# Heads of an RWKV-7 trunk: three waits placed anew (a maximum, a wait for a Newton step, a one-column sigmoid)

## The chip, the core and the metric
One core of one Trainium2 chip runs the whole program. The metric is the device time of one execution in microseconds (us); of several runs the median is taken. PE is the matrix engine (TensorE), DVE is VectorE, ACT is ScalarE, POOL is GpSimd, SP only issues DMAs.

## What is computed
Two layers (DEPTH = 2) of a trunk run over 544 tokens, 512 of a prompt and 32 of a second request. Of each layer this matters here:

```python
x = LN1(ALPHA*x + 0.5*swiglu_1(x))
u, z = split(x @ w_in)                    # z: r, k, v of 12 heads x 64, and low-rank inputs
w = -softplus(-(w0 + tanh(lw) @ w2)) - 0.5; decay = exp(-exp(w)); a = sigmoid(a0 + la @ a2)
kk = k*k_k; kk = kk / max(sqrt(sum(kk*kk)), 1e-12)      # key norm, per head
for t: S = S*w_t + (S a_t) b_t + v_t k_t;  y_t = S r_t     # state update, in chunks of 64 tokens
y = layer_norm(y per head) ...; out = (y + bonus) * g
x = LN2(ALPHA*x + [pool | out] @ w_out)
x = LN3(h + sigmoid(h W_g + b_g)*(p W_ple)), h = ALPHA*x + 0.5*swiglu_2(x)
```

The change lies in the part between `z` and `out`, the heads.

## The kernel before
Everything is kept with channels on the 128 partitions and tokens along the free dimension. Each engine runs its own instruction list, in order, and the lists meet in semaphores; the order in a list is written out by hand. `dense` does the large products (L519), weight slot by weight slot, with POOL splitting each slot into two fp32r parts (L462, L464). Between the products `z` and `wo` stands `heads`.

The 12 heads go in 6 pairs, and every pair p passes through `half_a(p)` and `half_b(p)`, each of ten slots k. In a slot an engine does a piece each of several works that run interleaved: the twelve `step`s (A, H1, H2, G16, X1, X2, X3, E64, V1, V2, V3, OUT) that build the chunk matrices of group 0 (chunks of the first half of the tokens) or group 1, where PE multiplies (L575) into PSUM and DVE (L1322) or, for G16, E64 and OUT, ACT (L979) copies out what the next step reads; the walk of the state over the chunks (`chunk_in` L603, `um` L1333, `chunk_out` L622, the carried part `Sd` by ACT L985, the new state `S` by DVE L1349, `chunk_y` L663); the preparation of the next pair (`prepare_1`, `prepare_2`); and the output norm of the pair before (`normalise`). The 6 pairs are written as pair 0, a loop `Fori(0, NPAIR - 2)` whose four passes do pairs 1 to 4, and pair 5, with a tail behind it. In half_a of pair p, group 1 of pair p-1 ends (V and OUT steps, and chunks 4 to 8) while group 0 of pair p begins.

Three places matter.

Key norm. In `half_a` slot 1 ACT scales and squares the key (L912, L914) and takes the first sigmoid (L918) of PE's low-rank product (L534); PE then makes the second low-rank product into the same banks, ACT its sigmoid (L921), then four exponentials of the scan `Lb` (L925 to L928). At slot 3 PE sums the squares (L534 again), and at slot 4 DVE writes the maximum with 1e-24 into `nv`, which is the tile `Lb` (L1257), behind the eviction of H1. ACT takes the reciprocal root of it (L933), POOL refines it (L389 to L399). PE, at slot 5, waits for `kkn_max` ahead of `chunk_in`, since both use bank 5. The orders are:

```python
IN_A = {0: (0,), 1: (1,), 2: (2,), 3: (3, 4), 4: (5,), 9: (10,)}   # pieces of prepare_1 in half_a
```

Output norm. In `half_b` slot 4 DVE runs `newton` (L1173, L1175, L1177) for the pair before, which first reads banks 5 and 6; POOL multiplies (L423), ACT applies gain and bias (L952) in slot 5. PE waits at slot 5 for the first of the three Newton operations, `hn_newton`, and for `bonus_ready`. chunk_in does nothing for chunk 0.

Activation tables. ACT's functions sit in tables; a change between sigmoid, exponential and reciprocal root puts an ACT_TABLE_LOAD in its list. Each loop pass has three, at L918, L925 and L933; Copy, Identity and Square need none.

Of the kernel before, what the change touches and what calls it, by code (L numbers as in the profile page):

```python
# [9 lines left out]
ACT = mybir.ActivationFunctionType  # L10
ALU = mybir.AluOpType

P = 128
# [60 lines left out]
def build(nc, xT, pT, w1i, w1o, wz, wo, w2i, w2o, wg, wp, params, consts, poolw, lora_w, g2_w,  # L74
          pool_hist, shift_hist, wkv_hist, y_out, pool_out, shift_out, wkv_out):
    ctx = ExitStack()
    with ctx:
# [7 lines left out]
        def sb(name, shape, dt=F32):  # L85
            t, top[0] = at(name, shape, dt, top[0])
            return t
# [16 lines left out]
        pool_hs = sb("pool_hs", [P, DEPTH, 2, HIST])  # L104
        last_z = sb("last_z", [P, NSH, 2])
        eps = sb("eps", [P, 2])
        lora_all = sb("lora_all", [P, DR])
        g2_all = sb("g2_all", [P, DR])
        lora_st = sb("lora_st", [P, P])
# [89 lines left out]
        def sem(name):  # L199
# [30 lines left out]
        ar_ready, bk_ready, vc_ready, rp_ready, rkk_ready, rk_mm, bonus_ready = (  # L230
            sem(n) for n in ("ar_ready", "bk_ready", "vc_ready", "rp_ready", "rkk_ready", "rk_mm", "bonus_ready"))
# [249 lines left out]
        def _(pe):  # L481
            pe.sem_inc(slot_used, 2)

            def constants_there():

                pe.wait_ge(loaded, 16 * NLOAD)
# [138 lines left out]
            def state_y(c, l, p):  # L625

                n = l * NPAIR + p
                if c == 0:
                    return
                o, rows = (64 * (c % 2), CH) if c < NCH else (0, TS)  # L630
                due, due_r = pe.to_reg(n * 5 + c // 2 if c % 2 == 0 else n * 4 + c // 2 + 1), pe.to_reg(n + 1)
                constants_there()
                if c == 4:
                    pe.wait_ge(rp_ready, due_r)
                if c % 2 == 0:

                    pe.wait_ge(yw_ready, due)
                else:
                    pe.wait_ge(ye_mm, due)
                st = S[c % 2] if c < NCH else Ss[0]  # L640
                for h in range(2):
                    hs = blk(h)
                    mm = pe.matmul(ps[hs, 7, o:o + rows], st[hs, :], ar[hs, 1, c * CH:c * CH + rows] if c < 4 else rp[hs, c * CH - 256:c * CH - 256 + rows],
                                   start=(c % 2 == 0), stop=True, skip_group_check=True)
                mm.then_inc(ys_mm, 1)
# [142 lines left out]
            def half_b(l, p, nxt, norm_before):  # L788
                n = l * NPAIR + p
                for k in range(SLOTS_B):  # L790
                    if k < 5:
                        step(7 + k, 0, n)
                    elif k < 9:
                        if k == 5:

                            due, due_bonus = pe.to_reg((n - 1) * 3 + 1 if norm_before else n + 2), pe.to_reg(n + 2)
                            constants_there()
                            if norm_before:
                                pe.wait_ge(hn_newton, due)
                            if nxt:  # L800
                                pe.wait_ge(bonus_ready, due_bonus)
                        chunk_in(k - 5, l, p)
                    if k == 0:
                        token_major(2, n, [])
                    elif k == 1:
                        token_major(3, n, [])
                        token_major(4, n, [])
                    elif k == 2:
                        products(1, n)
                    else:  # L810
                        step(k - 3, 1, n)
                    if 5 <= k < 9:
                        state_y(k - 5, l, p)
                        chunk_out(k - 5, l, p)
                        chunk_y(k - 5, l, p)
                    for q in IN_B.get(k, ()) if nxt else ():
                        prepare_2(l, p + 1, q, False)
                    if norm_before:
                        normalise(l, p - 1, k, nxt, True)
# [29 lines left out]
        def _(act):  # L849
# [152 lines left out]
            def half_a(l, p, left, right, nxt):  # L1002
                n = l * NPAIR + p
                for k in range(SLOTS_A):
                    if right and k < 5:
                        step(7 + k, 1, n - 1)
                    if right and k == 4:
                        sample_state(l, p - 1)
                    if right and 5 <= k < 9:
                        carry(k - 1, l, p - 1)  # L1010
                    if left and k < 2:
                        token_major(k, n)
                    if left and k >= 3:
                        step(k - 3, 0, n)
                    if right and k in (6, 8, 9):
                        y_tile({6: 2, 8: 3, 9: 4}[k], l, p - 1)
                    for q in IN_A.get(k, ()) if nxt else ():
                        prepare_1(l, p + 1, q, not right)
                if not left:

                    act.wait_ge(s_ready, n * 8)
                    act.wait_ge(ss_done, n)
                    for q, st in enumerate((S[0], Ss[1])):
                        act.dma_start(wkv_out[bass.ds(n - 1, 1), q, :, :].rearrange("a p v -> p (a v)"), st[:, :]).then_inc(wkv_stored, 16)
# [96 lines left out]
        def _(dve):  # L1121
# [118 lines left out]
            def prepare_1(l, p, k, first):  # L1240
                n = l * NPAIR + p
                r_ = row(zs, p)
                if k == 0:

                    dve.wait_ge(wa_mm, n * 2)
                    dve.tensor_copy(lora_st[:, :], lora_all[:, bass.ds(p * P, P)]).then_inc(staged, 1)
                if k == 2:
                    if not first:

                        dve.wait_ge(po_ready, n - 2)  # L1250
                    dve.wait_ge(sig_ready, n * 2 + 1)
                    dve.tensor_tensor_scan(Lb[:, :], const("reset"), tB[:, :], 0.0, ALU.mult, ALU.add).then_inc(scan_ready, 1)
                if k == 5:

                    dve.wait_ge(decay_ready, n * 4 + 4)
                    dve.wait_ge(kkn_mm, n + 1)
                    dve.tensor_scalar(halves(nv[:, :]), pair_bank(5), 1e-24, None, ALU.max).then_inc(kkn_max, 1)  # L1257
                if k == 10:
                    dve.wait_ge(kkb_ready, n + 1)
                    dve.wait_ge(kp_ready, n + 1)  # L1260
                    dve.scalar_tensor_tensor(tA[:, :], r_, col(l, p + COL["r_k"]), tB[:, :], ALU.mult, ALU.mult).then_inc(rkk_ready, 1)
# [33 lines left out]
            def products(g, n):  # L1295
                masks, lower = (const(name).rearrange("p (a t) -> p a t", a=3) for name in ("mt", "am"))
                for h in range(2):
                    us = slice(4 * g + h, 4 * g + h + 3, 2)
                    src = ps[:, 3 + h, :].rearrange("p (j t) -> p j t", j=2)
                    dve.wait_ge(am_mm, n * 5 + 3 * g - g + h + 1)  # L1300
                    dve.tensor_tensor(mt[:, :, us, :], src[:, :, 0:64].unsqueeze(1).to_broadcast([P, 3, 2, 64]),
                                      masks.unsqueeze(2).to_broadcast([P, 3, 2, 64]), ALU.mult)
                    dve.tensor_tensor(am[:, us, :, :], src[:, :, 64:256].rearrange("p j (a t) -> p j a t", a=3),
                                      lower.unsqueeze(1).to_broadcast([P, 2, 3, 64]), ALU.mult).then_inc(am_ready, 1)
                if g == 1:
                    dve.wait_ge(am_mm, n * 5 + 5)
                    dve.tensor_tensor(mt[:, :, 8, :], ps[:, 2, 0:64].unsqueeze(1).to_broadcast([P, 3, 64]), masks, ALU.mult)
                    dve.tensor_tensor(am[:, 8, :, :], ps[:, 2, 64:256].rearrange("p (a t) -> p a t", a=3), lower, ALU.mult).then_inc(am_ready, 1)
# [42 lines left out]
            def half_a(l, p, left, right, nxt):  # L1351
                n = l * NPAIR + p
                for k in range(SLOTS_A):
                    if right and k < 5:
                        step(7 + k, 1, n - 1)
                    if right and k >= 5:
                        chunk_in(k - 1, n - 1)
                    if left and k == 2:
                        products(0, n)
                    if left and k >= 3:  # L1360
                        step(k - 3, 0, n)
                    if right and k >= 5:
                        chunk_out(k - 1, l, p - 1)
                    for q in IN_A.get(k, ()) if nxt else ():
                        prepare_1(l, p + 1, q, not right)

            def half_b(l, p, nxt, norm_before):
# [184 lines left out]
```

## Time and profile before

| | us |
|---|---|
| median of 3 runs | 3031.05 |
| lowest, highest | 3028.4, 3035.96 |
| the profiled execution's own time | 3029.19 |
| its span, first to last instruction | 3027.2 |

PE is busy 2735.7 us of the span (90%), weight loads 2623.4, POOL 1445.2, DVE 1092.2, ACT 696.9. Busy shares are means over stages with different limits. Rows of a timeline give start and duration in us, the engine, line and operation, what was written from what, and in brackets the idle time of the engine just before, with what ended it. "issue" is a wait for nothing that the profile shows. PEclk 1.00 is the higher of TensorE's two levels (2.4 GHz), 0.50 the lower (1.2 GHz).

### The profile page before, as it was taken

What the parts mean: (1) busy time and instruction counts of PE and PEld (TensorE: products, weight loads), DVE (VectorE), ACT (ScalarE), POOL (GpSimd) and SP (SyncE); (2) the same over time, 40 slices, a digit from 0 to 9 for tenths busy, and PEclk for the clock granted to TensorE, in tenths of its full rate; (3) what the DMA queues carried; (4) which work ended last, traced back from release to release, by engine and by line L of the source; (5) the groups of instructions that cost most, each with busy time, mean ns of one, the idle gap of its engine ahead of it and who ended that gap; (6) DMA issues with size and microseconds to landing.
All of it is one profiled execution on the core that took longest, in us unless ns stands there. A gap on an engine that the chain in (4) does not pass through costs nothing.

```text
span 3027.2 us, 68787 instructions
## 1 busy us (share of the span) xinstructions
PE 2735.7 (90%) x27640; PEld 2623.4 (87%) x27640; DVE 1092.2 (36%) x1448; ACT 696.9 (23%) x1193; POOL 1445.2 (48%) x932
## 2 busy tenths in 40 slices
PE   8999989888887899999799999898888888999995
PEld 8999979776776799999699999797777777999994
DVE  3222047545553422211432210575545434222124
ACT  3221021233421322200232210212343203221013
POOL 5555645422213455555555555454222145555553
PEclk9999999889997999999999999898999989999997
DMA  4232322100001132332222322120000012223321
GB/s 147 88 90 82 89 60 85 36 3 4 3 19 43 56 90 83 97 86 77 85 73 87 90 85 85 60 84 22 4 3 4 17 57 63 90 85 93 90 73 57
DMA packets 64112, 192.66 MB, mean 64 GB/s; under 512 B 11712, under 2 KB 14016, under 8 KB 63936
## 3 DMA queue, kind: packets, MB, share of 16 engines
q1 hardware_dynamic: 59904, 185.95, 20.5%
q10 hardware_dynamic: 4032, 4.08, 0.4%
q8 instruction: 145, 2.38, 0.3%
q14 instruction: 31, 0.25, 0.0%
HBM read 186.88 MB, written 3.12 MB: 63 GB/s over the span
## 4 chain that ended last, share of the span: by engine, by line
PE 73%; issue 14%; POOL 6%; DVE 4%; ACT 3%; DVEq 0%; ACTq 0%; DMA 0%; POOLq 0%; SPq 0%
PE ps L519 64%; PE ps L575 4%; PE ps L534 2%; POOL w_lo L464 1%; DVE xl L1192 1%; PE ps L679 1%; POOL w_hi L462 1%; DVE y L1188 1%; DVE rs L1177 0%; POOL nt L391 0%; POOL tA L397 0%; POOL Lb L423 0%; POOL nt L389 0%; PE ps L694 0%; ACT xh L887 0%
## 5 line engine op out<-in xcount | busy, mean ns | idle before, releaser
L519 PE MATMUL ps<-xh,w_hi 128*128 128x272 f32 x4032 | 848.7, 292 | 104.3 <-POOL w_lo L464 49.0
L464 POOL TENSOR_TENSOR w_lo<-w_raw,w_hi 128x1024 fp32r<-128x1024 f32 (+3 forms) x380 | 854.8, 2249 | 31.7
L519 PE MATMUL ps<-xh,w_lo 128*128 128x272 f32 x4032 | 838.7, 290 | 0.0
L519 PE MATMUL ps<-xl,w_hi 128*128 128x272 f32 x4032 | 838.4, 290 | 0.0
L462 POOL TENSOR_SCALAR w_hi<-w_raw 128x1024 fp32r<-128x1024 f32 (+3 forms) x380 | 374.0, 984 | 865.7 <-PE ps L519 856.4
L519 PEld LDWEIGHTS ps<-xh,w_hi 128*128 128x128 f32 x4032 | 639.2, 190 | 118.4 <-DVE xl L1192 54.9
L519 PEld LDWEIGHTS ps<-xl,w_hi 128*128 128x128 f32 x4032 | 640.8, 191 | 0.0
L519 PEld LDWEIGHTS ps<-xh,w_lo 128*128 128x128 f32 x4032 | 636.3, 190 | 0.0
L1144 DVE TENSOR_TENSOR hf<-sg,ps 128x544 f32<-128x544 f32 x88 | 63.5, 722 | 708.3 <-PE ps L519 708.3
L519 PE MATMUL ps<-hh,w_hi 128*128 128x272 f32 x1472 | 305.5, 289 | 0.0
L519 PE MATMUL ps<-hl,w_hi 128*128 128x272 f32 x1472 | 303.6, 287 | 0.0
L519 PE MATMUL ps<-hh,w_lo 128*128 128x272 f32 x1472 | 303.3, 287 | 0.0
L519 PEld LDWEIGHTS ps<-hl,w_hi 128*128 128x128 f32 x1472 | 232.2, 188 | 0.0
L519 PEld LDWEIGHTS ps<-hh,w_hi 128*128 128x128 f32 x1472 | 229.8, 188 | 0.0
L519 PEld LDWEIGHTS ps<-hh,w_lo 128*128 128x128 f32 x1472 | 229.8, 188 | 0.0
L1146 DVE TENSOR_TENSOR hl<-hf,hh 128x544 f32 x88 | 197.7, 2246 | 83.5 <-ACT hh L874 83.5
L1160 DVE SCALAR_TENSOR_TENSOR y<-ps,y 128x544 f32 x48 | 34.8, 725 | 502.8 <-PE ps L519 502.8
L871 ACT ACT_TABLE_LOAD x88 | 112.9, 1283 | 361.6 <-PE ps L519 361.5
L874 ACT ACTIVATE hh<-hf 128x544 f32 x88 | 58.0, 659 | 444.1 <-DVE hf L1144 444.1
L881 ACT ACTIVATE sqs<-y 128x544 f32<-128x544 f32 x48 | 30.5, 658 | 388.2 <-DVE y L1182 388.2
L385 POOL TENSOR_TENSOR tB<-zs,tB 128x544 f32<-128x544 f32 x12 | 16.0, 1337 | 209.3 <-ACT tB L930 209.3
L423 POOL TENSOR_TENSOR Lb<-Lb,prs 128x544 f32<-128x544 f32 x12 | 16.0, 1333 | 178.0 <-DVE prs L1177 178.0
(242 smaller groups left out, 3202.8 us busy)
## 6 DMA issues: line engine op xcount, KB each, us to landing
w_raw<-in_w1i SPq DMA_DIRECT2D x88, 512.0 KB, 3.5
w_raw<-in_w2i SPq DMA_DIRECT2D x88, 512.0 KB, 3.5
w_raw<-in_wz SPq DMA_DIRECT2D x44, 512.0 KB, 3.5
w_raw<-in_w1o SPq DMA_DIRECT2D x32, 448.0 KB, 3.4
w_raw<-in_w2o SPq DMA_DIRECT2D x32, 448.0 KB, 3.3
w_raw<-in_w1o SPq DMA_DIRECT2D x16, 512.0 KB, 3.5
w_raw<-in_wo SPq DMA_DIRECT2D x16, 512.0 KB, 3.6
w_raw<-in_w2o SPq DMA_DIRECT2D x16, 512.0 KB, 3.5
```

Source lines behind the costliest of these rows:

```text
L462: pool.tensor_scalar(w_hi[k][:, 0:nk, :], w_raw[k][:, 0:nk, :], 1.0, 0.0, ALU.mult, ALU.add).then_inc(w_hi_done, 1)
L464: pool.tensor_tensor(w_lo[k][:, 0:nk, :], w_raw[k][:, 0:nk, :], w_hi[k][:, 0:nk, :].bitcast(F32), ALU.subtract).then_inc(w_split, 1)
L519: mm = pe.matmul(ps[:, 2 * pair + h, 0:HT], w[:, j, :], x[:, k0 + j, h * HT:(h + 1) * HT], start=(part == 0 and j == 0 and q == 0), stop=( ...
L534: mm = pe.matmul(ps[:, bank + h, 0:HT], lhsT, r[:, h * HT:(h + 1) * HT], start=start, stop=stop)
L575: mm = pe.matmul(ps[r, b, o + 64 * i:o + 64 * i + x.shape[-1]], lhsT, x, start=True, stop=True, skip_group_check=True)
L679: mm = pe.transpose(ps[:, 3 + j % 2, q * P:(q + 1) * P], src[:, j * P:(j + 1) * P], const("ident"))
L871: act.activation(halves(sg[:, :]), pair_bank(0), ACT.Silu).then_inc(tile_out[0], 1)
L874: act.activation(row(hh, m), hf[:, :], ACT.Copy).then_inc(hh_ready, 1)
L881: act.activation(sqs[:, m, :], y[:, m, :], ACT.Square).then_inc(sq_ready, 1)
L1144: dve.tensor_tensor(halves(hf[:, :]), halves(sg[:, :]), pair_bank(2), ALU.mult).then_inc(tile_out[1], 1)
L1146: dve.tensor_tensor(row(hl, m), hf[:, :], row(hh, m).bitcast(F32), ALU.subtract).then_inc(hl_ready, 1)
L1160: dve.scalar_tensor_tensor(halves(row(y, 2 * m + k)), pair_bank(2 * k), scale, halves(row(y, 2 * m + k)), ALU.mult, ALU.add).then_inc(tile ...
```

## The change
A tile `early` of one column is added. ACT writes it in slot 0 of half_a, of every pair behind which another stands, with a Sigmoid of one column. In DVE's half_a the piece 5 of prepare_1 (the maximum) stands in slot 4 ahead of the step's eviction instead of behind it. In PE's half_b, slot 5, the waits for `hn_newton` and `bonus_ready` stand behind the step (H2 of group 1) instead of ahead of it. No other operation is added or taken out.

```diff
--- before.py
+++ after.py
@@ -104,6 +104,7 @@
         pool_hs = sb("pool_hs", [P, DEPTH, 2, HIST])
         last_z = sb("last_z", [P, NSH, 2])
         eps = sb("eps", [P, 2])
+        early = sb("early", [P, 1])
         lora_all = sb("lora_all", [P, DR])
         g2_all = sb("g2_all", [P, DR])
         lora_st = sb("lora_st", [P, P])
@@ -791,14 +792,6 @@
                     if k < 5:
                         step(7 + k, 0, n)
                     elif k < 9:
-                        if k == 5:
-
-                            due, due_bonus = pe.to_reg((n - 1) * 3 + 1 if norm_before else n + 2), pe.to_reg(n + 2)
-                            constants_there()
-                            if norm_before:
-                                pe.wait_ge(hn_newton, due)
-                            if nxt:
-                                pe.wait_ge(bonus_ready, due_bonus)
                         chunk_in(k - 5, l, p)
                     if k == 0:
                         token_major(2, n, [])
@@ -810,6 +803,14 @@
                     else:
                         step(k - 3, 1, n)
                     if 5 <= k < 9:
+                        if k == 5:
+
+                            due, due_bonus = pe.to_reg((n - 1) * 3 + 1 if norm_before else n + 2), pe.to_reg(n + 2)
+                            constants_there()
+                            if norm_before:
+                                pe.wait_ge(hn_newton, due)
+                            if nxt:
+                                pe.wait_ge(bonus_ready, due_bonus)
                         state_y(k - 5, l, p)
                         chunk_out(k - 5, l, p)
                         chunk_y(k - 5, l, p)
@@ -1002,6 +1003,8 @@
             def half_a(l, p, left, right, nxt):
                 n = l * NPAIR + p
                 for k in range(SLOTS_A):
+                    if nxt and k == 0:
+                        act.activation(early[:, :], eps[:, 0:1], ACT.Sigmoid)
                     if right and k < 5:
                         step(7 + k, 1, n - 1)
                     if right and k == 4:
@@ -1357,11 +1360,13 @@
                         chunk_in(k - 1, n - 1)
                     if left and k == 2:
                         products(0, n)
+                    if nxt and k == 4:
+                        prepare_1(l, p + 1, 5, not right)
                     if left and k >= 3:
                         step(k - 3, 0, n)
                     if right and k >= 5:
                         chunk_out(k - 1, l, p - 1)
-                    for q in IN_A.get(k, ()) if nxt else ():
+                    for q in IN_A.get(k, ()) if nxt and k != 4 else ():
                         prepare_1(l, p + 1, q, not right)
 
             def half_b(l, p, nxt, norm_before):
```

## Rows read from the trace of the kernel before
**Rows 1.** The page, part 4: the chain that ended last, by engine

```profile
PE 73%; issue 14%; POOL 6%; DVE 4%; ACT 3%; DVEq 0%; ACTq 0%; DMA 0%; POOLq 0%; SPq 0%
```

**Rows 2.** Windows (from:to, length, busy each, PEclk, DMA, GB/s): pairs 0, 1, 2; 0, 4

```profile
588.90:642.60 53.70, 44.11 (x684) 36.84 (x684) 22.43 (x42) 17.07 (x37) 12.41 (x10) 0.69 0.01 2
642.60:694.80 52.20, 43.62 (x896) 37.62 (x896) 28.43 (x59) 22.61 (x53) 15.32 (x12) 1.00 0.02 4
694.80:750.20 55.40, 45.94 (x916) 39.55 (x916) 28.36 (x58) 22.91 (x53) 15.30 (x12) 0.97 0.02 4
2090.50:2141.20 50.70, 41.08 (x684) 34.44 (x684) 22.45 (x43) 17.12 (x37) 12.38 (x10) 0.77 0.01 2
2304.50:2360.80 56.30, 48.13 (x936) 41.34 (x936) 28.40 (x59) 23.20 (x54) 15.31 (x12) 0.94 0.02 3
```

**Rows 3.** Lines L918, L1257, L1173, who waited for each: us, times

```profile
  PE ps L534: 3.2, 8
...
  PE ps L603: 11.1, 8
...
  PE ps L575: 12.6, 10
```

**Rows 4.** Timeline, pair 1 of layer 0, half_a, slots 1 to 3

```profile
647.57 1.28 ACT L918 ACT_TABLE_LOAD   x1
...
648.86 0.71 ACT L918 ACTIVATE tB<-ps,par 128x544 f32<-128x544 f32 x1
...
649.63 1.18 PE L534 MATMUL ps<-lora,lora_st 64*128 64x272 f32 x4 [0.42 <-ACT tB L918]
...
653.07 0.69 DVE L1322 TENSOR_TENSOR zr<-ps,cst 128x512 f32<-128x512 f32 x1
```

**Rows 5.** Timeline, the same half_a, slots 3 to 5

```profile
652.96 1.18 PE L534 MATMUL ps<-tA,cst 128*128 128x272 f32 x4
...
654.25 0.19 ACT L928 ACTIVATE dec<-Lb 128x1 f32 x1
...
655.81 0.45 ACT L979 ACTIVATE b<-ps 128x320 f32<-128x320 f32 x1
...
655.90 0.42 DVE L1322 TENSOR_TENSOR b<-ps,cst 128x256 f32<-128x256 f32 x1 [2.14 <-PE ps L575]
...
656.24 0.71 DVE L1257 TENSOR_SCALAR Lb<-ps 128x544 f32<-128x544 f32 x1
...
657.25 0.33 PE L603 MATMUL ps<-S,wt 64*64 64x64 f32 x4 [1.39 <-DVE Lb L1257]
...
658.51 0.33 ACT L985 ACTIVATE Sd<-S,dec 128x64 f32<-128x64 f32 x1
...
659.28 0.28 DVE L1349 SCALAR_TENSOR_TENSOR S<-ps,dec,Sd 128x64 f32<-128x64 f32 x1
```

**Rows 6.** Timeline, pair 1 of layer 0, half_b, slots 4 to 6

```profile
681.61 0.49 DVE L1322 TENSOR_TENSOR b<-ps,cst 128x320 f32<-128x320 f32 x1 [1.78 <-PE ps L575]
...
682.84 0.34 PE L575 MATMUL ps<-mt,b 64*64 64x64 f32 x4 [1.26 <-DVE tA L1173]
...
686.00 0.84 ACT L952 ACTIVATE tA<-Lb,par 128x544 f32<-128x544 f32 x1 [4.15 <-POOL Lb L423]
...
686.75 0.33 ACT L985 ACTIVATE Sd<-S,dec 128x64 f32<-128x64 f32 x1
...
687.33 0.28 DVE L1349 SCALAR_TENSOR_TENSOR S<-ps,dec,Sd 128x64 f32<-128x64 f32 x1 [0.96 <-ACT Sd L985]
```

**Rows 7.** Timeline, ACT, slot 0 of half_a, pair 1 of layer 0

```profile
642.29 0.44 ACT L979 ACTIVATE b<-ps 128x320 f32<-128x320 f32 x1 [2.89 <-PE ps L575]
```

**Rows 8.** Timeline, pair 0 of layer 1, half_a, slots 3 and 4

```profile
2102.59 1.59 PE L534 MATMUL ps<-tA,cst 128*128 128x272 f32 x4
...
2104.84 0.42 DVE L1322 TENSOR_TENSOR b<-ps,cst 128x256 f32<-128x256 f32 x1 [1.45 <-PE ps L575]
```

**Rows 9.** Timeline, PE, first product of a loop pass behind a turn

```profile
696.15 0.80 PE L575 MATMUL ps<-mt,tz 64*64 64x64 f32 x20 [3.54 <-issue]
```

## The prediction
> **What bounds the kernel now.** I read first the page's chain of what ended last: PE holds 73% of it, and 14% is issue time [rows 1]. Most of that is the large products, which the change doesn't touch. So only `heads` can move, and the next view is the table of windows over the pairs, cut where DVE writes the last piece of `ar`. A pair takes 50.7 to 56.3 us [rows 2]; 12 pairs are some 650 us of 3027. In a pair with both halves at work PE is busy 43.6 of 52.2 us, and no engine is full: what counts there is a chain of handovers, PE to DVE or ACT and back. One microsecond taken out of that chain is one microsecond of the program; one taken from beside it is nothing. The last views are who waited for the three lines that the change touches [rows 3], and the timeline around each [rows 4 to 8]. The reader should look there at each row's start, at start plus duration of the row that released it, and above all at the second-latest arrival, since it becomes the last.
>
> How often: the norm of pair p+1 is prepared in half_a of pairs 0 to 4. PE's waits for the sigmoid and for the maximum are eight each, pairs 1 to 4 of two layers, 0.40 and 1.39 us a time. The wait for the Newton step is ten, 1.26 a time [rows 3]. I work out pair 1 of layer 0; the other seven repeat its rows within 0.2 us.
>
> **The early sigmoid.** It adds one column, at most the 0.19 us of the one-column exponential L928 [rows 5], and moves ten table loads of 1.28 us [rows 4] to slot 0. There they are 1.47 us. ACT sits idle for 2.89 us before E64's eviction, waiting for PE [rows 7], the shortest such place: behind a loop turn PE is late by another 3.54 us [rows 9]. So 1.42 us of cover are left, and nothing is paid; without that cover it would be 1.47 us a pair. The new instruction waits for no semaphore. What it frees: the first sigmoid starts at 647.57 instead of 648.86, and ends by 648.3. PE can't use all of it. Its second low-rank product starts at 649.63 after 0.42 us of idle time, so PE's own queue was full until 649.21 [rows 4]. The gain is 0.40 us a pair (rows 3's mean), not 1.28. It goes on: the second sigmoid follows PE, the exponentials follow that, and A's product, the norm's sum, OUT and H1 on PE stand in line behind. DVE's scan doesn't move, because it stands behind the product evictions, but it leaves DVE free in time for A's eviction at 653.07 [rows 4]. By slot 4 all is 0.40 earlier.
>
> The Trainium skill (ScalarE: Activation LUTs, section What ACT_TABLE_LOAD costs) puts a drain of about 1380 ns on top of the load's 1283 ns, 2.66 us a switch. The trace disagrees: the load starts at 647.57, and the sigmoid runs at 648.86, 1.29 us later [rows 4], with no drain behind it. By the page load and column would fill 2.85 of the 2.89 us of cover, and with a tenth or two of slip in pair 1 the sum would be 4.4 us instead of 4.6.
>
> **The maximum ahead of H1's eviction.** No operation is added. DVE idles 2.14 us before that eviction at 655.90, then takes 0.42 for it and 0.71 for the maximum, and PE starts `chunk_in` of chunk 4 at 657.25 after 1.39 us of idle time [rows 5]. The maximum waits for the norm's sum on PE (652.96 + 1.18 = 654.14) and the last exponential (654.25 + 0.19 = 654.44) [rows 5]. Minus 0.40 these are 653.74 and 654.04, so it can run from about 654.15 to 654.86, within the idle time. Behind it in DVE's list waits H1's eviction, ready at 655.50: 0.64 us of cover. If the maximum were released later than 654.8, each microsecond would delay H2 on PE and all that follows.
>
> What is late next for PE? `chunk_in` 4 also needs OUT's eviction by ACT, 655.81 + 0.45 = 656.26 [rows 5], minus 0.40 is 655.86. With 0.1 to 0.3 us of handover PE starts at about 656.05, 1.2 us earlier. But the next state doesn't follow by 1.2. Its update S (659.28) needs `Sd` from ACT, which stands in ACT's list behind the load and reciprocal root of the norm; these follow OUT's eviction without a gap, so they are only 0.40 earlier. Sd ends at 658.51 + 0.33 - 0.40 = 658.44 [rows 5]. From Sd's end (686.75 + 0.33 = 687.08) to S (687.33) another place shows 0.25 us [rows 6]. S then starts at 658.69 instead of 659.28: **0.59 us earlier**, of which 0.19 belongs to the maximum. From there chunks 5 to 8 repeat S, `chunk_in`, `um`, `chunk_out` with a PE in step, and I carry 0.59 through to the next half. POOL's chain of the norm ends early and has no one waiting in this half.
>
> Bounds for the maximum's share: 0 from below, if Sd's handover is slower than 0.44; above, what PE gains, 1.2 - 0.40 = 0.8 us. I take 0.19, since S can't run without Sd. In pair 0 PE has no such wait. In layer 1 the norm's sum ends at 2102.59 + 1.59 = 2104.18 and H1's eviction starts at 2104.84 [rows 8]; the maximum in front may run to 2105.0, which costs 0.15 us once. In layer 0 the lower clock gives PE's H1 more time, and nothing is lost. The early sigmoid gives nothing in pair 0, where PE never waited for that line (eight waits in all, none in pair 0) [rows 3].
>
> **The wait behind H2.** PE starts H2 of group 1 at 682.84, held by the first Newton operation; its input, H1's eviction, is there at 681.61 + 0.49 = 682.10 [rows 6]. So H2 and what stands behind it on PE come 0.5 to 0.6 us earlier; behind it the moved wait finds its count reached. But DVE evicts H2 only after all three Newton operations, which stand ahead in its own list. And the state of chunk 1 waits at 687.33 for Sd (0.96 us), Sd stands in ACT's list behind L952 (686.00), and that waited 4.15 us for POOL, which waits for the last Newton operation [rows 6]. DVE, POOL and ACT don't see the move. I cost it at 0, with bounds of 0 and 0.55. A loss has no mechanism, since nothing is put in front of anything that waits.
>
> **Sum.** 8 x 0.59 = 4.72, minus 0.15: 4.6 us. The profiled execution took 3029.19 us, 1.86 below the median, with 2.0 around its span; it would take 3024.6, the median 3026.4. A measurement here can tell about 0.3%, 9 us, from no change, so I expect a gain too small to tell.
>
> **Rivals.**
> 1. **The moved wait does pay.** If the handovers behind H2 carry PE's 0.55 us in all ten places, 5.5 us come on top: 3020.9. For it speaks the largest wait of the three in total, 12.6 us; against it ACT's place behind POOL. Chance 0.08.
> 2. **The load stays.** If the compiled list still has a load ahead of L918, the early one is for nothing, and only the maximum's 0.19 is left: 8 x 0.19 = 1.5, 3029.5. No function between the two places needed a load before, so this is unlikely: 0.06.
> 3. **The clock takes it back: slower than before.** Pair 0 takes 53.7 us with a mean granted clock of 0.69 in layer 0 and 50.7 with 0.77 in layer 1; a loop pass takes 56.3 with 0.94 and 55.4 with 0.97 [rows 2]. The lower level follows PE's idle stretches, the one at the loop turn of 3.54 us among them [rows 9], and the change moves where these fall. With layer 1's pair 0 as in layer 0 (+3.0) and the six passes that start with a loop turn as the slow one (+0.9 each, 5.4) it is 8.4 us on 3026.4: 3034.8. It decides from 4.6 us on. For it: the three runs already differ by 7.6 us. Against: less idle time, not more, is left in front of PE. Chance 0.12.
> 4. **The clock gives.** Layer 0's pair 0 goes as in layer 1: 3.0 less, 3023.4. Chance 0.12.
>
> My forecast has the remaining 0.62. The range goes from 3019 to 3034: it takes in rivals 1, 2 and 4 and most of 3, and the bounds 0 and 0.8 of the maximum's share (8 x 0.6 = 4.9 on the early side gives 3021.5). Faster by over 0.3% is below 3022.0: most of rival 1 and a corner of 4, 0.11. Slower by over 0.3% is above 3040.1: only rival 3 with more on top, 0.03. Within: 0.86.
>
> **What would show it.** In the profile after, L918 has no table load and the line of the one column has ten; PE's wait for the first sigmoid is gone, and the second sigmoid starts 0.2 us behind PE as before. The maximum stands between A's and H1's evictions, H1's idle time falls from 2.14 to about 0.6 us, and L603 waits no more for L1257 but for ACT. S of chunk 4 waits for Sd, and the pair 1 window is 51.6 instead of 52.2 us. In half_b PE's 1.26 us before H2 fall to about 0.7, while S of chunk 1 keeps its distance to the Newton operations. The forecast is wrong if S of chunk 4 goes with PE (then Sd wasn't last), if H1's eviction comes late (then the maximum's releases were later than read), or if the windows of equal clock don't differ by 0.6 us.

## The result, and the profile after

The changed kernel takes 3012.32 us (median of 4 runs, 3010.99 to 3015.53) against 3030.44 for the kernel before (4 runs, 3028.4 to 3035.96): ratio 0.9939, 95% interval 0.9923 to 0.9955, so 14 to 23 us faster. Forecast were 3026.4 us and a range down to 3019. In a second comparison (below) it took 3017.7 us, ratio 0.9967, 0.9955 to 0.9979, or 6 to 14 us faster. The gain is real, both times larger than the forecast 4.6 us, and its size differs between comparisons; why is half of the story.

First the rows that answer to the forecast's. The page's chain (part 4) of the changed kernel, beside [rows 1]:

```profile
PE 71%; issue 16%; POOL 7%; DVE 4%; ACT 2%; DMA 0%; DVEq 0%; ACTq 0%; POOLq 0%; SPq 0%
```

Who waited for the line of the first sigmoid (now L919), what the one-column line L1007 does, and what DVE waited for ahead of the maximum (L1260): [rows 3] had eight waits for L918 and eight for L1257.

```profile
L1007 ACT ACT_TABLE_LOAD  x10: 1283/1283/1283, 584.9 to 2286.5; - x10
L1007 ACT ACTIVATE early<-eps x10: 202/203/203, 586.2 to 2287.8; 128x1 f32<-128x1 f32 x10
...
  ACT dec L929: 6.4, 8
```

The ten loads have moved, nobody waits for L919 any more, and the maximum waits 0.80 us a time for the last exponential, as worked out. The timeline of pair 1 of layer 0, half_a, beside [rows 5]:

```profile
645.62 0.71 ACT L922 ACTIVATE aa<-ps,par 128x544 f32<-128x544 f32 x1 [2.37 <-PE ps L535]
...
649.17 0.72 DVE L1260 TENSOR_SCALAR Lb<-ps 128x544 f32<-128x544 f32 x1 [0.80 <-ACT dec L929]
...
650.50 0.42 DVE L1325 TENSOR_TENSOR b<-ps,cst 128x256 f32<-128x256 f32 x1 [0.61 <-PE ps L576]
...
650.96 0.33 PE L604 MATMUL ps<-S,wt 64*64 64x64 f32 x4 [0.50 <-issue]
...
653.11 0.33 ACT L986 ACTIVATE Sd<-S,dec 128x64 f32<-128x64 f32 x1
...
653.71 0.28 DVE L1352 SCALAR_TENSOR_TENSOR S<-ps,dec,Sd 128x64 f32<-128x64 f32 x1 [0.61 <-ACT Sd L986]
...
654.14 0.33 PE L604 MATMUL ps<-S,wt 64*64 64x64 f32 x4 [1.05 <-DVE S L1352]
```

H1's eviction comes 0.61 us after the maximum, undelayed. `chunk_in` of chunk 4 starts 0.46 us behind that eviction instead of 1.35, and 1.2 us sooner behind the pair's start, as forecast. The next state S now waits 0.61 us for ACT's Sd, and PE gets 1.05 us of idle time back there. Before, S stood directly behind another entry of DVE's own list, H2's eviction, and Sd had ended 0.44 us ahead of it (658.51 + 0.33 = 658.84 against 659.28). That row of the kernel before, in which DVE waited for PE, is:

```profile
658.67 0.69 DVE L1322 TENSOR_TENSOR tq<-ps,cst 128x512 f32<-128x512 f32 x1 [0.77 <-PE ps L575]
```

In the changed kernel Sd ends at 653.44 and S starts at 653.71, 0.27 us later. In half_b of the same pair, beside [rows 6]:

```profile
676.70 0.34 PE L576 MATMUL ps<-mt,b 64*64 64x64 f32 x4 [0.68 <-DVE b L1325]
...
680.45 0.84 ACT L953 ACTIVATE tA<-Lb,par 128x544 f32<-128x544 f32 x1 [4.15 <-POOL Lb L424]
...
681.78 0.28 DVE L1352 SCALAR_TENSOR_TENSOR S<-ps,dec,Sd 128x64 f32<-128x64 f32 x1 [1.34 <-ACT Sd L986]
```

H2 starts 0.6 us sooner (PE idles 0.68 us ahead of it, 1.26 before), L953 waits the same 4.15 us, and S's wait for Sd grows from 0.96 to 1.34 us: the time given comes back as a wait. So much went by the forecast. But the windows, beside [rows 2] (busy time of PE, PEld, DVE, ACT and POOL, then the clock; pairs 0, 1, 2 of layer 0, the stretch from pair 5 to the first `wo` residual, then pairs 0, 1 and 4 of layer 1), don't differ by 0.6 us alone:

```profile
586.90:637.60 50.70, 41.00 (x684) 34.08 (x684) 22.59 (x44) 17.33 (x38) 12.46 (x10) 0.78 0.01 2
637.60:689.20 51.60, 43.66 (x896) 37.66 (x896) 28.29 (x58) 22.52 (x54) 15.31 (x12) 1.00 0.02 4
689.20:743.50 54.30, 45.95 (x916) 39.58 (x916) 28.33 (x58) 22.90 (x54) 15.31 (x12) 0.97 0.02 4
...
853.00:945.50 92.50, 68.34 (x1183) 58.89 (x1184) 41.06 (x77) 22.12 (x62) 15.58 (x11) 0.85 0.09 26
2077.30:2126.60 49.30, 39.73 (x684) 33.51 (x684) 22.40 (x42) 17.28 (x38) 12.38 (x10) 0.80 0.01 2
2126.60:2180.60 54.00, 46.16 (x896) 40.11 (x896) 28.37 (x59) 22.59 (x54) 15.31 (x12) 0.94 0.02 4
...
2289.50:2343.90 54.40, 46.88 (x936) 40.36 (x936) 28.34 (x58) 21.71 (x53) 15.32 (x12) 0.97 0.02 4
```

The same stretch behind pair 5 in the kernel before:

```profile
860.20:958.40 98.20, 74.20 (x1183) 63.79 (x1184) 41.17 (x77) 22.23 (x62) 15.58 (x11) 0.77 0.09 25
```

Pair 1 of layer 0, at clock 1.00 in both, is 0.5 us shorter (52.15 to 51.66 between the two starts of DVE's last piece). Pair 0, which the change hardly touches, is 3.1 us shorter with 0.78 for 0.69, and the stretch behind pair 5 is 5.7 us shorter with 0.85 for 0.77. Those 5.7 us need not be the change's work: in layer 1 the same stretch takes 92.5 us before and 93.1 us changed, so the kernel before has the short form too. The spans differ by 16.6 us (3027.2 and 3010.6), and the eight passes of pairs 1 to 4 can give 4 of them.

### The profile page after: what moved, and what is told of

Its sections match the earlier page's. It is cut to its first block, busy times and chain, and to the rows that moved or that the text cites. A ratio compares the mean times of both kernels' runs of the same rounds, so it can differ in the third digit from the quotient of the medians.

```text
span 3010.6 us, 68805 instructions
## 1 busy us (share of the span) xinstructions
PE 2725.3 (91%) x27640; PEld 2614.1 (87%) x27640; DVE 1091.5 (36%) x1448; ACT 696.8 (23%) x1203; POOL 1446.5 (48%) x932
## 3 DMA queue, kind: packets, MB, share of 16 engines
q8 instruction: 144, 2.36, 0.3%
## 4 chain that ended last, share of the span: by engine, by line
PE 71%; issue 16%; POOL 7%; DVE 4%; ACT 2%; DMA 0%; DVEq 0%; ACTq 0%; POOLq 0%; SPq 0%
PE ps L520 63%; PE ps L576 3%; PE ps L535 3%; POOL w_lo L465 1%; DVE xl L1195 1%; POOL w_hi L463 1%; PE ps L680 1%; PE ps L695 1%; DVE y L1191 1%; POOL Lb L424 1%; POOL nt L392 0%; POOL tA L398 0%; POOL nt L390 0%; ACT xh L888 0%; DVE rs L1180 0%
```

## The experiments

"Low time" of a run is the time that PE was granted its lower level (1.2 GHz): 2 x (1 - mean granted clock) x time. Its price can be read where two profiles have the same work and another clock. Pair 0 of layer 0 took 53.7 us at 0.69 [rows 2] and 47.9 at 0.84 (kernel `e10`, below); with the exact stretches 33.2 and 15.7 us of low time, (53.72 - 47.85) / (33.2 - 15.7) = 0.33 us per us. The stretch behind pair 5 gives (98.21 - 92.53) / (44.4 - 27.3) = 0.33 again. Neither needs the change: pair 0 has the same 47.85 us in `e7`, where no instruction moved, and the 92.53 us stand in layer 1 of the kernel before, with 27.3 us of low time. Over whole runs the price is lower: a straight line through the 69 runs of the kernel before (all comparisons below) gives 0.25 us per us. I use 0.33, and say where 0.25 would matter.

**One part alone.**

```diff
 # e1_early: of the change, only these lines
+        early = sb("early", [P, 1])
+                    if nxt and k == 0:
+                        act.activation(early[:, :], eps[:, 0:1], ACT.Sigmoid)
```

> The one-column sigmoid and its tile alone. Theory of handovers: PE's 0.40 us wait for the first sigmoid goes eight times, 3.2 us less than before (3027); PE's wait for the maximum stays at 1.39 us. Rival, the addresses: the new tile moves all tiles allocated after it by 32 bytes, and 10 us or more of the 18 come with it, here and with the tile alone. Rival, the clock: what lies beyond 3.2 us comes from shorter stretches at the lower level in pair 0 and in the tail of the heads, seen in the granted clock of the windows.

Measured: 3017.2 us (12 runs), ratio 0.9968 (0.9955 to 0.9980), against 3027.73 in 35 runs. 9.7 us, not 3.2. In its profile PE's wait for the maximum stays (the columns as above):

```profile
651.10 0.43 DVE L1325 TENSOR_TENSOR b<-ps,cst 128x256 f32<-128x256 f32 x1 [2.14 <-PE ps L576]
...
652.45 0.33 PE L604 MATMUL ps<-S,wt 64*64 64x64 f32 x4 [1.39 <-DVE Lb L1260]
...
654.51 0.27 DVE L1352 SCALAR_TENSOR_TENSOR S<-ps,dec,Sd 128x64 f32<-128x64 f32 x1
```

The mean granted clock of its runs, 0.9549, is that of the 35 before (0.9547). So most of the surplus isn't the clock's; the run with the tile alone (`e4`, below) shows whose.

```diff
 # e2_max: DVE's half_a as in the change, nothing else
+                    if nxt and k == 4:
+                        prepare_1(l, p + 1, 5, not right)
-                    for q in IN_A.get(k, ()) if nxt else ():
+                    for q in IN_A.get(k, ()) if nxt and k != 4 else ():
```

> The maximum ahead of H1's eviction, alone. Theory of handovers: S of chunk 4 waits for Sd, 0.19 us earlier eight times, 1.5 us less than before (3029), and H1's eviction isn't delayed. If PE's 0.8 us counted in full it would be 6 to 7 us less. Rival, the clock: more than that with a higher granted clock in pair 0, though no instruction of PE is touched there.

Measured: 3028.55 us (12 runs), ratio 1.0004 (0.9991 to 1.0016): nothing that can be told from no change, and the 1.5 us expected lie inside the interval too. Its profile has no more low time in all than that of before (269 and 272 us), but more of it in the passes, as the windows of pairs 3 and 4 of layer 0 show:

```profile
747.50:802.70 55.20, 46.10 (x916) 39.66 (x916) 28.57 (x58) 22.93 (x53) 15.34 (x12) 0.97 0.02 4
802.70:859.90 57.20, 49.13 (x936) 42.71 (x936) 28.59 (x58) 23.24 (x54) 15.34 (x12) 0.91 0.02 3
```

Three of its six passes behind a loop turn have a second stretch at the lower level, behind the S of chunk 4, and are 2 us longer; the profile of before has none of these. That the maximum brings them isn't shown: `e4` and `e11` below, which move no instruction, have one each.

```diff
 # e3_wait: PE's half_b as in the change; W = the wait for hn_newton and bonus_ready
-                        W                       # ahead of chunk_in and the step H2
+                        W                       # behind the step, ahead of state_y
```

> PE's wait behind H2, alone. Theory of handovers: 0, 3030, since the last Newton operation, POOL, ACT and Sd set the next state. Rival 1 of the prediction (the moved wait pays): 5.5 us less, 3025. If the missing 14 us are the clock's, and H2 half a microsecond earlier changes what PE does in the stretch before the clock is granted anew, 10 us or more less.

Measured: 3030.18 us (12 runs), ratio 1.0017 (1.0007 to 1.0026): 2 to 8 us slower. By handovers it is worth nothing, as the profile shows: H2 starts behind H1's eviction, and S waits for Sd as long as in the changed kernel.

```profile
678.57 0.34 PE L575 MATMUL ps<-mt,b 64*64 64x64 f32 x4 [0.68 <-DVE b L1322]
...
683.64 0.28 DVE L1349 SCALAR_TENSOR_TENSOR S<-ps,dec,Sd 128x64 f32<-128x64 f32 x1 [1.33 <-ACT Sd L985]
```

Its clock, 0.9523, is the lowest of all, 289 us of low time against 274; 15 x 0.33 = 5.0 us (3.7 at 0.25), as large as the loss of 5.1 by the ratio. The medians of all runs, 3030.18 and 3027.73, differ by 2.5 us.

**The tile itself.**

```diff
 # e4_pad: allocated, never written
+        early = sb("early", [P, 1])
```

> Only the tile of one column is allocated, and nothing is written into it. Theory of handovers and the clock: no change, 3030. Rival, the addresses: 10 us or more less, from moving the tiles by 32 bytes.

Measured: 3023.2 us (12 runs), ratio 0.9988 (0.9977 to 0.9999). A tile that nobody uses makes the program faster, by less than the 10 us that I had written down for it. Everything allocated behind it moves by 32 bytes, the feed-forward tiles `hh` and `hl` among them, which PE reads in the second products. One of these products, 1056 matmuls, took 132.49 us from its first start to its last before, and 131.3 to 131.9 here; another, 1152 matmuls with the embedding's among them, took 200.28 and 199.1 to 199.3. All four together: 665.5 us before, 661.6 here, 661.1 in the changed kernel. It can be read from one row, the stretch from 300 to 400 us, where PE does nothing but the second product. Before, changed, and three kernels that follow (`e6`, `e7`, `e11`):

```profile
300.00:400.00 100.00, 100.00 (x798) 100.00 (x798) 8.70 (x12) 0.00 (x0) 60.53 (x37) 1.00 0.30 87
```

```profile
300.00:400.00 100.00, 100.00 (x806) 100.00 (x805) 8.70 (x12) 0.00 (x0) 60.93 (x37) 1.00 0.30 87
```

```profile
300.00:400.00 100.00, 100.00 (x799) 100.00 (x798) 8.70 (x12) 0.00 (x0) 60.28 (x37) 1.00 0.30 87
```

```profile
300.00:400.00 100.00, 100.00 (x806) 100.00 (x805) 8.70 (x12) 0.00 (x0) 60.68 (x37) 1.00 0.30 87
```

```profile
300.00:400.00 100.00, 100.00 (x798) 100.00 (x798) 8.70 (x12) 0.00 (x0) 60.35 (x37) 1.00 0.30 87
```

798 matmuls in 100 us against 806, both at full clock with PE never idle. Each of the two products of 1056 matmuls is 1.2 us shorter in the changed kernel, and each of the two of 1152 is 1.0 to 1.1 us shorter: that is where 4.4 of 665 us come from.

**The changed kernel again, and without its move of the tiles.**

> The changed kernel once more, in more runs. By parts: 4 us for the addresses (the second products of the feed-forward parts took 665.5 us before and 661.1 in the changed kernel's profile), 4 us for the handovers (8 x 0.5), and what the clock gives, 4 to 8 us: 3012 to 3016 against some 3027. If the first comparison was luck of the clock, 3019.

Measured: 3017.7 us (6 runs), ratio 0.9967 (0.9955 to 0.9979) against 3029.45 (23 runs). That lies between the two times expected; how much the first comparison owed to the clock comes below.

```diff
 # e6_unshifted: the changed kernel
-        eps = sb("eps", [P, 2])
-        early = sb("early", [P, 1])
+        eps = sb("eps", [P, 3])
-                        act.activation(early[:, :], eps[:, 0:1], ACT.Sigmoid)
+                        act.activation(eps[:, 2:3], eps[:, 0:1], ACT.Sigmoid)
```

> The changed kernel, but the one column is written into a spare third column of the tile eps, so no tile moves. Theory of the addresses: 4 us more than the changed kernel, and the four second products sum to 665.5 us again. Without it: the same time as the changed kernel.

Measured: 3020.3 us (12 runs), ratio 0.9976 (0.9965 to 0.9986). Its second products sum to 665.5 us, the slow value to the tenth; the difference in total, 2.6 us, is short of 4.4; its runs had the higher clock (0.9561 against 0.9553), which at 0.33 accounts for 1.4 us of that.

```diff
 # e7_gap64: the kernel before
+        gap = sb("gap", [P, 16])        # behind eps: 64 bytes
```

> The kernel before with an unused tile of 64 bytes behind eps. If it is the start of hh and hl at 32 bytes behind a multiple of 64 that costs, it is left so here: no change, 665.5 us for the second products, about 3027. If any move of the tiles helps, 3023 as with 32 bytes.

Measured: 3019.77 us (12 runs), ratio 0.9975 (0.9965 to 0.9984), second products 661.1 us. My guess about multiples of 64 bytes fell: 32 and 64 bytes help alike.

```diff
 # e11_gap_behind: the kernel before
+        gap = sb("gap", [P, 8])         # ahead of sg, behind hl
 # e12_gap_between: the kernel before
+        gap = sb("gap", [P, 8])         # ahead of hl, behind hh
```

> The kernel before with 32 unused bytes behind hl, so that of the feed-forward tiles only sg, hf, sq, rs and ysum move. If where hh and hl stand sets the speed of the second products, these stay at 132.5 and 200.3 us. If it is DVE's and ACT's tiles, they fall to 131.3 and 199.1.

> The kernel before with 32 unused bytes between hh and hl: hl moves against hh. If it counts where hh stands, 132.5 and 200.3 us stay. If hl's place counts, or the distance of the two, the second products change.

One run each: 3025.1 and 3027.3 us, second products 665.5 and 665.6 us. The tiles of DVE and ACT behind hl don't matter, nor does hl alone. All seven kernels in which hh and what stands ahead of it moved have the fast value (661.1 to 663.1 us), all six in which hh stays have 665.5 or 665.6. It is hh's place, or that of a tile allocated between eps and it; why, these runs don't show. Nor is it the place alone that sets the last microsecond: two profiles of the changed kernel have 661.1 and 662.0.

**Is Sd what holds the state?**

```diff
 # e8_sd_first: the changed kernel; ACT, half_a
                     if right and 5 <= k < 9:
                         carry(k - 1, l, p - 1)
+                    if right and nxt and k == 5:
+                        prepare_1(l, p + 1, 5, False)
-                    for q in IN_A.get(k, ()) if nxt else ():
+                    for q in IN_A.get(k, ()) if nxt and not (right and k == 4) else ():
```

> The changed kernel with ACT's load and reciprocal root of the norm moved from slot 4 to slot 5, behind Sd of chunk 4. If Sd is what S of chunk 4 waits for, S comes with PE, 0.6 us earlier in eight places, 5 us less than the changed kernel by handovers; the norm's chain on POOL starts 0.3 to 0.6 us later, and no one waits for it. If something else holds S, or the clock takes it back as it did with the maximum alone, no gain.

Measured: 3014.86 us (5 runs), ratio 0.9955 (0.9943 to 0.9968). And the changed kernel and `e8`, each with PE's wait back in its old place:

```diff
 # e9_early_max: the changed kernel with W ahead of chunk_in and H2 again
 # e10_sd_first_nw: e8_sd_first with W ahead of chunk_in and H2 again
```

> The changed kernel with PE's wait put back ahead of H2: early sigmoid, its tile and the maximum are left. By the handovers the moved wait is worth 0, so this is the changed kernel's time, 3015 to 3018. If the wait alone loses by the clock (it did, 3030.2 against 3027.7 with the mean granted clock 0.952 against 0.955), this is up to 5 us faster, 3011 to 3013, with less time at the lower level than the changed kernel.

> As the one before, and ACT's load and reciprocal root of the norm stand behind Sd of chunk 4. By handovers 5 us less than the one before. With the wait moved this kernel spent 7 us in a loop pass at the lower level where the changed one spent 3.4; if the wait was the cause, 3.4 us stand here too and the time is 3008 to 3010; if earlier work of PE in half_a is the cause, the 7 us stay and the time is 3013 to 3015.

Measured: 3015.48 us (6 runs), ratio 0.9955 (0.9939 to 0.9971), and 3015.01 us (6 runs), ratio 0.9953 (0.9936 to 0.9969). That `e9` beats the changed kernel (3017.7) isn't shown: the intervals overlap. In `e10` the six passes behind a loop turn hold 3.4, 3.5, 3.6, 6.4, 6.8 and 7.0 us at the lower level, so neither of the two causes written down decides them. Sd is out of the way of S there; S again follows H2's eviction, and that follows PE:

```profile
648.84 0.35 ACT L986 ACTIVATE Sd<-S,dec 128x64 f32<-128x64 f32 x1
...
649.21 1.28 ACT L934 ACT_TABLE_LOAD   x1
...
650.13 0.69 DVE L1327 TENSOR_TENSOR tq<-ps,cst 128x512 f32<-128x512 f32 x1 [0.80 <-PE ps L576]
...
650.74 0.28 DVE L1354 SCALAR_TENSOR_TENSOR S<-ps,dec,Sd 128x64 f32<-128x64 f32 x1
...
651.16 0.33 PE L604 MATMUL ps<-S,wt 64*64 64x64 f32 x4 [0.35 <-DVE S L1354]
```

From the second sigmoid to this S are 7.4 us in all eight passes of e8 and e10, 8.1 in those of the changed kernel, e2 and e9, and 8.3 in those of before, e1 and e3. So Sd did hold S, and 0.7 us a pass come free, 5.8 us together. The total didn't follow by as much. The windows of e10, for pairs 0 and 1 of layer 0 and the stretch behind pair 5:

```profile
587.40:635.30 47.90, 38.24 (x684) 31.93 (x684) 22.58 (x43) 17.33 (x38) 12.47 (x10) 0.84 0.01 2
635.30:686.20 50.90, 43.58 (x896) 37.61 (x896) 28.29 (x58) 22.64 (x54) 15.33 (x12) 1.00 0.02 5
...
849.20:946.20 97.00, 72.70 (x1183) 62.58 (x1184) 41.20 (x76) 22.28 (x62) 15.60 (x10) 0.79 0.09 25
```

Pair 1 is 0.7 us shorter than in the changed kernel, but the stretch behind pair 5 has 0.79 instead of 0.85 and is 4.5 us longer; over both layers of e8 and e10 it is 3 to 4.5 us longer. `e11`, which moves no instruction, has the same long form in layer 0 (96.5 us), so that the move of Sd causes it isn't shown. e8 and e10 are the fastest medians of their comparisons; from the changed kernel and e9 these runs can't tell them.

**The account.** Three terms, each from a row: 4.4 us where hh moved; the handovers as the passes show them; 0.33 us for each us of low time more or less than in the runs of before of the same comparison.

| kernel | place of hh | handovers | clock (low time) | sum | measured (ratio x 3028, interval) |
|---|---|---|---|---|---|
| e1 early | -4.4 | -2.6 | -0.7 (272, 274) | -7.7 | -9.7 (-13.6 to -6.1) |
| e2 max | 0 | -1.3 | +1.0 (277, 274) | -0.3 | +1.2 (-2.7 to +4.8) |
| e3 wait | 0 | 0 | +5.0 (289, 274) | +5.0 | +5.1 (+2.1 to +7.9) |
| e4 tile | -4.4 | 0 | +1.7 (279, 274) | -2.7 | -3.6 (-7.0 to -0.3) |
| e5 changed | -4.4 | -3.9 | -2.6 (269, 277) | -10.9 | -10.0 (-13.6 to -6.4) |
| e6 unshifted | 0 | -3.9 | -4.0 (265, 277) | -7.9 | -7.3 (-10.6 to -4.2) |
| e7 64 bytes | -4.4 | 0 | -2.3 (270, 277) | -6.7 | -7.6 (-10.6 to -4.8) |
| e8 Sd first | -4.4 | -9.7 | +3.3 (287, 277) | -10.8 | -13.6 (-17.3 to -9.7) |
| e9 early, max | -4.4 | -3.9 | -6.3 (260, 279) | -14.6 | -13.6 (-18.5 to -8.8) |
| e10 | -4.4 | -9.7 | +1.3 (283, 279) | -12.8 | -14.2 (-19.4 to -9.4) |

All ten sums lie in their intervals, with 0.25 for the price as well. The intervals are 6 to 10 us wide: the table shows that the three terms are enough, not each of them to a microsecond. Their sizes rest on the rows. The first comparison's 18 us: 4.4 and 3.9, and a low time of 257.4 us in the changed kernel's four runs against 275.7 in 69 runs of before, 6.0 us. That makes 14.3; it lies within the interval of 14 to 23; 3.8 of the 18.1 are left over, and the before runs there stand 1.6 us above the median of the 69 (3028.8). At 0.25 the sum is 12.9, just outside the interval's end of 13.6.

## Why the prediction was wrong

**The early sigmoid.** Right in mechanism: ten loads moved under cover, PE's wait gone eight times, the second sigmoid 0.33 us earlier (8.40 to 8.07 us behind DVE's last piece in pair 1) where 0.40 was forecast. In pairs 2 to 4 the lower clock ahead of it hides the same distance; the shortest found there are 11.1 us without the early sigmoid and 10.7 with it. The trace's load without a drain held: the column starts 1.3 us behind its load (586.2 and 584.9).

**The maximum.** Right: inside DVE's idle time, H1's eviction undelayed, S held by Sd. The share was 0.16 to 0.17 us against 0.19, the two together 0.50 against 0.59: 3.9 us instead of 4.7, so each of the two shares was read 0.03 to 0.07 too large. The share is what Sd had in hand before (0.44 us) less the handover it needs (0.27, where I had read 0.25). That Sd was the limit in the changed kernel, and not PE, e8 and e10 showed by moving it. What the maximum alone couldn't give came with Sd out of the way: 0.17 and 0.7 us, 0.9 a pass. The 0.15 us set against it in pair 0 of layer 1 are there, as 0.22: H1's eviction starts 2.36 us behind A's, 2.14 before.

**The moved wait.** Right at 0 by handovers, against rival 1: from S of chunk 4 to the next pair's last piece are 35.5 to 35.7 us in every pass at full clock, with it and without it. "A loss has no mechanism" was wrong: e3 lost 2 to 8 us, with 15 us more of low time.

**What the sum left out.** I costed the new tile at nothing, without a term for it. The step that failed is "it adds one column": it also moves every tile behind it, and 4.4 us of the gain are that, as much as the handovers. No row of before shows it by itself, but the pace of the second products against the first ones (125.5 ns a matmul, and 125.0 from 100 to 200 us, PE busy all the time) was there to be asked about.

**The clock.** This is the other term that the sum put at nothing. Rivals 3 and 4 had the right mechanism, with 0.12 each, and prices from the two layers of one execution; for a gain that was 3.0 us, and the first comparison got 6.0 (the second 2.6). How much of that is the change's own can be estimated from the runs. The low time of the kernel before scatters by 14 us (standard deviation of the 69 runs), so a mean of 12 runs is good to some 4 us and one of 6 to some 6. Of the single kernels e3 stands clearest (15 us more, 3 times its error); e9 (19 less) and the changed kernel's first four runs (18 less) stand at 2.5 to 2.7 times, and its second comparison (8 less) at one. Together the 28 runs that have both the early sigmoid and the maximum, with Sd in its place (the changed kernel twice, e6, e9), have a mean of 264 us against 276, 3.7 times the error. So some 12 us of low time, 3 to 4 us of time, come with the change, and the rest of the first comparison's 6.0 was the luck of its runs. What decides the direction stays open: e3 had more low time, and so had e8 and e10 (10 and 4 us more, within the scatter), though they have the early sigmoid too.

**The range.** Handovers of 3.9 and the tile's 4.4 put the time at 3022.7 from the 3031.05 shown, and at 3020.5 from the 3028.8 that 69 runs of before have as their median; a clock term of 6.3 us to either side (e9's, the largest) makes 3016.4 to 3029.0, or 3014.2 to 3026.8. The second comparison's 3017.7 lies in both, the first's 3012.3 below both by 2 to 4 us. Mine ended at 3019: it had neither the tile, nor the clock, nor the 2 us by which the median of three runs stood off that of the 69.

## What to carry to other kernels

An allocation is part of a change: before a microsecond is credited to a moved instruction, run the kernel with the new tile and nothing else, and keep the added word in padding that exists. Where the granted clock of equal work differs between two profiles, or between two layers of one, price that first, over many runs; a chain argument good to a tenth of a microsecond says little about the total while the clock moves it by five. And where a releaser is taken away, look whose row ends next: here it was ACT's Sd behind a table load, and the next move (Sd first) was there to be read. It gave its 0.7 us a pass, though the total hasn't been shown to follow.

## What the hardware showed that I had not expected

Where tiles stand in SBUF (hh, or one between eps and it) changes the pace of the matmuls that read hh: 125.5 against 124.3 ns a matmul (132.49 us and 131.29 us for 1056), PE never idle, clock 1.00. Moves by 32 and by 64 bytes give the same. The time falls in steps of 0.6 us (132.49, 131.89, 131.29); the two lower ones occur in one and the same run (`e4`), the highest only where hh stays. Which tile ahead of or at hh it is, and why, wasn't tried further.

PE's branch back at a loop turn of the heads holds its queue 3.3 to 3.9 us in every profile (3.84, 3.55, 3.28 in layer 0 before; 3.38, 3.86, 3.69 changed), while its last branch, out of the loop, takes 0.08. Those six add up to 21.7 us in the kernel before, more than all that this change moved. A stretch at the lower level goes with every one of the 84 in the 14 profiles: it starts at the earliest 1.6 us ahead of the branch's end, and at the latest 2.0 us behind it.
